# A two-layer transformer block on one core: paired attentions normalised on POOL before the turn, inverses no longer turned

## The reference

```python
def gqa_attend(q, k, v, bias=None, sink=None):
    s = jnp.einsum("bqhgd,bkhd->bhgqk", q, k, preferred_element_type=jnp.float32) * ATTN_SCALE
    if bias is not None:
        s = s + bias
    if sink is not None:
        sink_col = jnp.broadcast_to(sink.astype(jnp.float32)[None, :, :, None, None], s.shape[:-1] + (1,))
        p = jax.nn.softmax(jnp.concatenate([s, sink_col], axis=-1), axis=-1)[..., :-1]
    else:
        p = jax.nn.softmax(s, axis=-1)
    return jnp.einsum("bhgqk,bkhd->bqhgd", p.astype(v.dtype), v)

# even_mixer: 8 heads "A" over all 768 tokens, 8 heads "B" in a band of 128 with sinks, 256 context tokens as well
y_lat = jnp.concatenate([oa * jax.nn.silu(ag), ob * jax.nn.silu(bg)], axis=-1) @ w_out
# odd_mixer: a gated convolution, and 8 heads "D" over 8 rows x 16 columns near the query, with a relative bias
y_lat = jnp.concatenate([oc, od * jax.nn.silu(dg)], axis=-1) @ w_out
```

## Time and profile before

| | us |
|---|---|
| median of 3 runs | 1742.69 (1741.37 to 1743.02) |
| the profiled execution | 1740.23, span 1738.9 |
| TensorE busy in the span | 1676.9 (96%) |
| DVE, ACT, POOL busy | 957.9, 737.2, 666.7 |
| chain that ended last | 87% TensorE, 6% DVE, 3% ACT |
| even attention | from 1126.7 to about 1346 |
| odd attention | from 1564.5 to about 1651 |

### The profile page before, as it was taken

One profiled execution on the slowest core, in us unless ns is written; L12 is line 12 of the kernel. 1 busy time (PEld: TensorE's weight loads), 2 busy tenths in 40 slices (PEclk: granted clock), 3 DMA queues, 4 the chain that ended last, 5 costly groups with the idle time before them and its releaser, 6 DMA issues.

```text
span 1738.9 us, 25645 instructions
## 1 busy us (share of the span) xinstructions
PE 1676.9 (96%) x9946; PEld 1369.3 (79%) x9946; DVE 957.9 (55%) x1977; ACT 737.2 (42%) x1469; POOL 666.7 (38%) x291
## 2 busy tenths in 40 slices
PE   8999999899999999999999999999999899999997
PEld 6789777688888888888878886777777788897776
DVE  4697545452232265555597223655666557985463
ACT  5222354552333454444423442265666225225553
POOL 3877322243334454444466412111113233522231
PEclk9999999999999999999999999999999999999998
DMA  8656312132224323333474321100000442321121
GB/s 244 178 162 170 91 49 73 39 108 85 73 86 142 101 56 108 97 96 98 138 205 136 110 65 41 49 26 26 14 26 2 121 132 73 95 73 43 44 73 49
DMA packets 255158, 156.35 MB, mean 90 GB/s; under 512 B 6017, under 2 KB 250942, under 8 KB 255038
## 3 DMA queue, kind: packets, MB, share of 16 engines
q1 hardware_dynamic: 251518, 147.12, 28.9%
q10 hardware_dynamic: 3520, 7.60, 1.3%
HBM read 152.60 MB, written 2.10 MB: 89 GB/s over the span
## 4 chain that ended last, share of the span: by engine, by line
PE 87%; DVE 6%; ACT 3%; issue 2%; POOL 1%; DMA 1%; ACTq 0%; DVEq 0%
PE ps L812 69%; PE ps L2461 3%; PE ps L2492 3%; PE ps L2475 2%; PE ps L1586 1%; DVE mod_sums L1533 1%; PE ps L1602 1%; PE ps L1548 1%; POOL w_lo L782 1%; DVE probsT L2572 1%; PE ps L1594 1%; ACT w_hi L723 1%; PE ps L2202 1%; DVE probs L2561 1%; PE ps L2496 0%
## 5 line engine op out<-in xcount | busy, mean ns | idle before, releaser
L782 POOL TENSOR_TENSOR w_lo<-w_raw,w_hi 128x1024 fp32r<-128x1024 f32 (+1 forms) x220 | 583.9, 2659 | 866.6 <-ACT w_hi L723 866.2
L812 PE MATMUL ps<-h_hi,w_lo 128*128 128x512 f32 x1088 | 436.9, 402 | 12.1 <-POOL w_lo L782 3.9
L812 PE MATMUL ps<-h_hi,w_hi 128*128 128x512 f32 x1088 | 424.8, 390 | 0.0
L812 PE MATMUL ps<-h_lo,w_hi 128*128 128x512 f32 x1088 | 424.5, 390 | 0.0
L812 PEld LDWEIGHTS ps<-h_hi,w_lo 128*128 128x128 f32 x1088 | 204.8, 188 | 63.2 <-POOL w_lo L782 7.1
L723 ACT ACTIVATE w_hi<-w_raw 128x1024 fp32r<-128x1024 f32 (+1 forms) x220 | 228.7, 1045 | 36.8 <-PE ps L812 20.1
L812 PEld LDWEIGHTS ps<-h_hi,w_hi 128*128 128x128 f32 x1088 | 204.6, 188 | 44.1
L812 PEld LDWEIGHTS ps<-h_lo,w_hi 128*128 128x128 f32 x1088 | 205.1, 189 | 40.9 <-issue 1.4
L2545 ACT ACTIVATE probs<-probs,small 128x512 f32<-128x512 f32 (+3 forms) x128 | 93.7, 732 | 28.3 <-DVE small L2561 27.4
L2572 DVE COPY probsT<-ps 128x256 f32<-128x256 f32 (+3 forms) x128 | 55.1, 430 | 68.5 <-PE ps L2475 68.0
L2042 ACT ACTIVATE conv<-ps,cols 128x512 f32<-128x512 f32 x44 | 34.3, 779 | 127.4 <-DVE ps L2133 127.4
(11 more groups left out here) (424 smaller groups left out, 3265.4 us busy)
## 6 DMA issues: line engine op xcount, KB each, us to landing
w_raw<-in_w_in SPq DMA_DIRECT2D x56, 512.0 KB, 5.2
mod_raw<-in_mod_w SPq DMA_DIRECT2D x24, 1024.0 KB, 5.7
w_raw<-in_w_up SPq DMA_DIRECT2D x44, 512.0 KB, 3.8
w_raw<-in_od_w_in SPq DMA_DIRECT2D x28, 512.0 KB, 3.7
w_raw<-in_ev_w_in SPq DMA_DIRECT2D x20, 512.0 KB, 3.8
w_raw<-in_w_down SPq DMA_DIRECT2D x16, 512.0 KB, 4.2
w_raw<-in_w_mem_kv SPq DMA_DIRECT2D x8, 512.0 KB, 4.1
w_raw<-in_w_attn_branch SPq DMA_DIRECT2D x8, 512.0 KB, 3.8
```

Source lines behind the costliest of these rows:

```text
L782: POOL.tensor_tensor(wlo[:, p, 0:n], raw[:, p, 0:n], f(whi[:, p, 0:n]), ALU.subtract).then_inc(*chunk_lo.by(c))
L812: ins = PE.matmul(out, l, r, start=first and n == 0, stop=last and n == 2)
```

## The change

1. POOL multiplies each half of `probs` by its inverse sum, in place in SBUF (`pool_scale`), and the turn waits for that (`p_scaled`) in place of the exponential.
2. DVE inverts each half by itself (`dve_invert`): half 0 behind the maximum of half 1, and half 1 behind the copy of the turned half 1 of the pair before. The sink's sum becomes two instructions as well.
3. The widening (`dve_widen`), its two transposes and ACT's copy (`act_inverse`) are gone; DVE scales the values in PSUM by 0.5 (`dve_out`). `inv_wide` has no memory any more.
4. POOL's order in both attentions is written by pair (`pool_even_attention`, `pool_odd_attention`): products, and behind certain pairs a chunk's low half, a gate's product, two biases.
5. Chunks of wo2, cg and wo3 are rounded one tile earlier, with one more rounding ahead of each of wo2 and cg (`act_round(first_chunk["wo2"] + 3)`, `act_round(first_chunk["cg"] + 3)`).
6. TensorE's wait for the last even gate stands before the first tile that uses the gate's bank, and its wait for the last attended tile of the odd attention behind the first cg tile.

```diff
@@ chunk table @@
-                if not (job == "qA" and c >= 3 or job == "up" and (c < 3 or c == 43) or job == "u0" and c == 3):
-                    round_after[job, u] = n_chunks + c + 3 + (job in ("qA", "up", "u0"))
+                if not (job == "qA" and c >= 3 or job == "up" and (c < 3 or c == 43) or (job, c) in (("u0", 3), ("wo2", 7))):
+                    round_after[job, u] = n_chunks + c + 3 + (job in ("qA", "up", "wo2", "u0", "cg", "wo3"))
@@ pe_turn, pe_values @@
-        PE.wait_ge(*p_exped(x_, p, s))
+        PE.wait_ge(*p_scaled(x_, p, s))
...
-        PE.wait_ge(*p_widened(x_, g))
-        for n in range(2):
-            ins = PE.transpose(bank(V_BANK, P, 2 * P + n * P), inv_wide[:, n, :], ident[:])
         ins.then_inc(*p_weighted.by(x_, g))
@@ act_pairs @@
-            if p >= 4 and p % 2 == 0 and p < n + 3:
-                act_inverse((p - 4) // 2, x_, us)
@@ dve_pairs @@
-            if 3 <= p <= n + 1 and p % 2:
-                dve_widen((p - 3) // 2, x_)
...
-                DVE.wait_ge(*p_exped(x_, p - 1, 1))
-                if "sink" in u:
-                    dve_step(DVE.tensor_tensor(total, total, esink, ALU.add))
-                    dve_after()
-                DVE.reciprocal(inv, total).then_inc(*p_inverted.by(x_, p - 1))
             if p < n:
                 dve_maximum(x_, p, us[p], 1, probs)
+                dve_invert(x_, p, us[p], 0)
             beside(p)
             if 1 <= p <= n:
                 copy(p - 1, 1)
+            if p < n:
+                dve_invert(x_, p, us[p], 1)
             yield
+    def dve_invert(x_, p, u, s):
+        _, total, inv, esink = [at[:, s:s + 1] for at in pair_stats(p)]
+        DVE.wait_ge(*p_exped(x_, p, s))
+        if "sink" in u:
+            dve_step(DVE.tensor_tensor(total, total, esink, ALU.add))
+            dve_after()
+        DVE.reciprocal(inv, total).then_inc(*p_inverted.by(x_, p, s))
+
+    def pool_scale(x_, p, u, probs):
+        for s in range(2):
+            S, inv = probs[s][p % 2][:, 0:u["n"]], pair_stats(p)[2][:, s:s + 1]
+            POOL.wait_ge(*p_inverted(x_, p, s))
+            POOL.tensor_tensor(S, S, inv.to_broadcast([P, u["n"]]), ALU.mult).then_inc(*p_scaled.by(x_, p, s))
 
     def dve_out(g, x_, us):
-        DVE.wait_ge(*p_inv_copied(x_, g))
-        DVE.tensor_tensor(us[2 * g]["out"], bank(V_BANK, 2 * P), us[2 * g]["out"], ALU.mult).then_inc(*p_attended.by(x_, g))
+        DVE.wait_ge(*p_weighted(x_, g))
+        DVE.tensor_scalar(us[2 * g]["out"], bank(V_BANK, 2 * P), 0.5, None, ALU.mult).then_inc(*p_attended.by(x_, g))
@@ POOL @@
+    def pool_even_attention():
+        for p in range(52):
+            if p < len(even_units):
+                pool_scale("E", p, even_units[p], probs2)
+            if p == 0:
+                pool_low(first_chunk["ag"] + 2)
+            if p >= 5 and (p - 5) % 6 == 0 and (p - 5) // 6 < len(GATED):
+                pool_low(first_chunk["ag"] + 3 + (p - 5) // 6)
+            if p >= 9 and (p - 9) % 6 == 0:
+                pool_gate_even((p - 9) // 6)
+            if p in (40, 41, 46):
+                pool_gated_low((40, 41, 46).index(p))
+
+    def pool_odd_attention():
+        for p in range(18):
+            if p < len(odd_units):
+                pool_scale("D", p, odd_units[p], probs3)
+            if p >= 5 and p % 4 == 1:
+                pool_low(first_chunk["dg"] + 3 + (p - 5) // 4)
+            if p in (6, 10):
+                for n in range(2):
+                    pool_bias((p + 2) // 4 * 2 + n)
+            if p in (7, 11, 15, 17):
+                pool_gate_odd((7, 11, 15, 17).index(p))
@@ pe_even_out @@
-        PE.wait_ge(*g_silu("bg", 3))
...
                     wait_bank("wo2", u)
-                b = ring_bank("wo2", u)
+                    if b + 4 == 6:
+                        PE.wait_ge(*g_silu("bg", 3))
@@ act_even_out, act_odd_out @@
+        act_round(first_chunk["wo2"] + 3)
...
+        act_round(first_chunk["cg"] + 3)
@@ pe_odd_out @@
-        PE.wait_ge(*p_attended("D", 7))
         next(cg)
         next(cg)
+        PE.wait_ge(*p_attended("D", 7))
```

More of the change, by code:

```diff
@@ L501, in build @@
     p_copied_act = signal("p_copied_act", halves)
-    p_inverted = signal("p_inverted", pairs)
+    p_inverted = signal("p_inverted", halves)
+    p_scaled = signal("p_scaled", halves)
     p_weighted = signal("p_weighted", outs)
-    p_widened = signal("p_widened", outs)
-    p_inv_copied = signal("p_inv_copied", outs)
     p_attended = signal("p_attended", outs)
@@ L723, in act_round, with pool_low @@
         ACTE.activation(whi[:, p, 0:n], raw[:, p, 0:n], ACT.Copy).then_inc(*chunk_hi.by(c))
+    def pool_low(c):
+        p, n = c % PLACES, CHUNKS[c][1] * CHUNKS[c][2]
+        POOL.wait_ge(*chunk_hi(c))
+        POOL.tensor_tensor(wlo[:, p, 0:n], raw[:, p, 0:n], f(whi[:, p, 0:n]), ALU.subtract).then_inc(*chunk_lo.by(c))
     def pool_windows():
@@ L774, in gpsimd_program @@
         means = pool_windows()
+        within = [first_chunk["ag"] + i for i in range(2, 11)] + [first_chunk["dg"] + i for i in range(3, 7)]
         for c in range(n_chunks):
+            if c in within:
+                continue
             if c == first_chunk["up"] + 4:
@@ L779, in gpsimd_program @@
                 pool_c(t)
[L780 to L782 removed]
+            pool_low(c)
             if c >= first_chunk["q"] + 4:
                 next(means, None)
[L785 to L791 removed]
+            for at, heads_ in (("dq", (0, 1)), ("dk", (2, 3))):
                 if c == first_chunk[at] + 2:
@@ L794, in gpsimd_program @@
                         pool_bias(head)
[L795 to L799 removed]
+            if c == first_chunk["ag"] + 1:
+                pool_even_attention()
+            if c == first_chunk["dg"] + 2:
+                pool_odd_attention()
     def chunk_views(c):
```

36 lines of the change are left out of this document (4 added, 32 removed).

## The result

The changed kernel took 1755.4 us (median of 4 runs, 1751.6 to 1758.9) against 1742.9 for the kernel before, run beside it: ratio 1.0077, 95% interval 1.0065 to 1.0089, so 12.5 us slower. The forecast was 1756. The profiled execution took 1751.6 us (span 1749.9), 11.3 more than the one of before. It is the fastest of the four; what follows splits this execution, not the median.

A forecast was written before the change was run, and what follows sets the result against it. TensorE's instruction order was taken to set the pace; -11.8 + 5.7 + 9.6 + 1.4 + 2.0 + 12.0 + 3.0 - 7.3 - 0.8 = +13.8 us on 1740.2 gave 1754.0, median 1756 us. Range 1732 to 1769.

The forecast's parts named there:

- 33.7 us of delays: Both attentions: TensorE's turns late behind POOL and DVE, plus slower clock after long idles; 33.7 us added.
- 11.8 removed: Both attentions, TensorE: two transposes of widened inverses gone, 0.37 us for each of 24 + 8 groups; 11.8 us.
- 1.1 and 0.45 us of lateness: Even attention without band: turns before wide pairs late by 1.1 us after a narrow pair, 0.45 after a wide one.
- upper bound: POOL's broadcast product, price taken from a scaling: 3.1 ns a column at most, some 16 us more.
- 9.6: Even attention, banded half with sinks: late turns of 2.4 us per six pairs, four times; 9.6 us.
- The chain of the prediction: From one turn through ACT's exponential, DVE's inverses, maxima and copy, and POOL's product to the turn 1.5 pairs later.
- The port: DVE instructions with two SBUF inputs and POOL instructions reading SBUF exclude each other for a whole instruction; more POOL work, more waits.
- rival 3: DVE's sums and POOL's products block each other, 0.2 on 48 sums; clock falls at three idles, 1.7 each; 1768 us; chance 0.16.
- Biases 4.9: Odd attention, pairs 6 and 10: two bias products on POOL before the next pair's products; 2.45 us each, 4.9 together.
- First seam: -7.3: After the even attention: gate wait -2.0, chunk wait -2.8, its clock loss -1.7, low-half wait -0.7; sum given as -7.3 us.
- Second seam: -0.8: After the odd attention: ACT copy and latencies leave the way to the last attended tile; gate tile's wait 0; -0.8 us.
- rival 1: Both attentions: POOL's products stay hidden, by cheap broadcast or looser orders; -18 us, 1725 us; chance 0.17.

The follow-up runs named there:

- short products: The changed kernel with POOL multiplying only the first 64 columns of each half's exponentials: 1740.0 us, 0.9982 of the kernel before.
- gate behind the copy: The changed kernel with DVE's two gate products moved behind the copy of the previous pair's turned half 1: 1759.5 us, 1.0085 of the kernel before.
- inverse later: The changed kernel with DVE's inverse of each pair's half 1 moved behind the next pair's maximum of half 0: 1761.5 us, 1.0105 of the kernel before.
- both seams alone: The kernel before with only the change's edits at the two output projections, attentions as before: 1738.0 us, 0.9983 of the kernel before.

## Why the prediction was right, and where its terms were off

The mechanism was right: TensorE gains from the missing transposes and loses more at turns that wait for POOL. Of the 33.7 us of delays in the two attentions some 28 came, if the 11.8 removed are taken as foretold. That the total came within 2 us is partly luck, since errors of 5.9 and 4.1 us cancel.

**Removed, 11.8.** No inverse is turned any more, and nothing else went from TensorE's queue: right. With the short products the 12 groups without band came out 2.8 us earlier, 0.24 a group, against my 0.37; some of it is then spent on waits of 0.2 us.

**Even attention, no band: +3.3 foretold (5.7 and 2.0, less 4.4), -1.0 measured.** Two terms were too large, in part through the product's price. At 1.47 us for 1.82 each chain is 0.35 us shorter. But the 1.1 and 0.45 us of lateness came out as waits of about 0.3 and 0.2, and from 1.1 to 0.3 the price explains less than half; the rest is slack between the steps that the sum didn't have. The start cost 0.6 in place of 2.0: pair 1 waited 0.5 us for its product. The 3.1 ns a column of the upper bound is real, but for the scaling form. The Trainium skill ("GPSIMD Engine Reference", Elementwise — side-by-side cycle accounting) prices two-input products at about 2.6 cycles an element, and bodies of at most two operations at 1.03. For 768 columns these are estimates of 1.66 and 0.66 us at the 1.2 GHz of its example. Measured were 1.47 us here and 1.83 for two full tensors, so neither figure gives it.

**Even attention, banded: +6.6 foretold (9.6 and 1.4, less 4.4), +6.1 measured.** Right in the total, with a mechanism only partly mine, and the two sizes are off against each other: the waits at the three gated lower halves come to 3.7 us, some 3.3 more than at the same turns of other sixes, where I had 1.4, so about 7 is left for the 9.6. The chain of the prediction is in the trace, but I took it for the only one. The run with the gate behind the copy shows another, DVE's copy, that ends 0.2 us from it, and the one with the inverse later shows that POOL's own queue, with its chunk half, is as late as the chain. The port, which I had covered, cost about 0.5 us in this order, as the sum written as a scaling shows; rival 3's price for it (0.2 on each of 48 sums) falls.

**Odd attention: +12.0 foretold (12.0 and 3.0, less 3.0), +10.9 measured.** The parts were shifted. The start's 3.0 was 2.7. Pairs 4 to 7, for which I took 3.5 for the port, cost 0.6 in two waits: the subtractions took 0.67 to 1.43 us, much as before, but the widening that had been blocked for 2.28 is gone, and with it 1.45 us of stall. Biases 4.9: two waits of 2.6, and 4.6 back with the clock when taken apart. The clock took 5.1 us where I had 3.0; that is rival 3's 1.7 at each of three idles, the one part on which it was right.

**First seam: -7.3 foretold (its terms add up to 7.2), -5.9 measured.** Both waits went, and the clock kept its speed, which it didn't in the two kernels with the old attentions (-4.5 and -4.4). 1.4 us came back at once, at the sums of the modulation (1.2 us for L1530), which the prediction had named as next in line and let pass because DVE was idle there.

**Second seam: -0.8 foretold, +1.9 measured.** The step that failed. I saw that TensorE would wait for the last gated lower half and put the 2.3 us at 0, but not that the edit lengthens that chain: the chunk rounded ahead stands on ACT before the gated halves (1.05 us), and the longer waits, 1.7 and 4.0, cost one more spell of low clock, 1.7 us. With the foretold -0.8 these make the +1.9: from the last values to the last gated tile's rounding the chain took 32.4 us before, 33.2 with both seams alone, and 32.5 in the changed kernel, where ACT's copy is gone.

**The sum.** +13.8 foretold, +12.0 measured: 4.3, 0.5 and 1.1 us too much at the attentions, 1.4 and 2.7 too little at the seams. The forecast held because the waits for POOL were read from the chain and not from POOL's share (72 us of 114 in the trace), which said that there was room. The signs that the prediction named held less well: POOL was busy 799 us, not 830, a product of 768 columns took 1.47 us, not 1.8, and TensorE waited 8.8 us for POOL in the even attention, not some 20, with 6.4 more for DVE's copies. It also named that attention 7 us longer, where the prediction's own terms add up to 9.9; it was 5.1. "Short products" is rival 1 made as real as an edit can, and it ends at 1740, not at the 1725 that I gave it. About half of these 15 us is the even attention, where even products of 0.3 us left most of what the transposes gave unused; the other half is the odd attention, where chunk halves and biases still hold POOL, and the two seams.

## What to carry over

Work moved to an idle engine costs its latency, not its share: between two steps that another engine takes in order, look for the slack at each step, and put nothing longer than that slack (here about 1.2 us against chunk halves of 2.4 and bias pairs of 3.6) in the same queue. Where two chains end within a few tenths of each other, mending one gives next to nothing. Before rounding or loading ahead, ask whether the instruction stands in the chain that the next stage waits for.

## What was new of the hardware

A POOL product with a broadcast column took 1.47 us for 768 columns and 0.61 for 256, 1.7 ns a column and 0.18 us a start; the same scaling by a scalar operand took 2.21 and 0.93, 2.5 ns a column; two full tensors 1.83 for 768. So the product with a broadcast column is a third cheaper than the scaling, and worth 29 us here.

A DVE sum of two SBUF columns took up to 1.37 us beside POOL in the changed kernel (2.25 with the inverse later), with one of them as the scalar operand never more than 0.22.
